# Score products of a recurrent mixer as tiles of 32 weight columns

## The chip, the cores and the metric

One NeuronCore of a Trainium2 chip runs the whole program. The metric is the device time of one execution in microseconds (us); the median of the runs counts. TensorE is called PE here, VectorE DVE, ScalarE ACT, GpSimd POOL, and SyncE SP.

## The reference, cut to what matters

Two transformer-like blocks run one after the other on 1024 tokens of 1024 features, all in fp32. The change touches one part of the first block, the HGRN2 mixer. It has 6 heads of 128 channels:

```python
# per chunk: b = cumsum(log_f); diff[t, s] = b[t] - b[s] for s <= t, else -inf
scores = jnp.einsum('bhtk,bhsk,bhtsk->bhts', qb, kb, jnp.exp(diff))
o = (jnp.einsum('bhts,bhsv->bhtv', scores, vb)
     + jnp.einsum('bhtk,bhkv->bhtv', qb * jnp.exp(b), state))
new_state = (jnp.exp(b_last[:, :, 0, :])[..., None] * state
             + jnp.einsum('bhsk,bhsv->bhkv', kb * jnp.exp(b_last - b), vb))
```

The score of a query token t and a key token s is a product over channels with the decay between s and t in it. Around the mixer stand the projection into it (w_in), a pooling mixer, the projection out (w_out) and an MLP; the second block has neighbourhood attention, a convolution and a gated MLP.

## The kernel before, in words

Activations are kept with features on the partitions and the 1024 tokens along the free axis. A projection is a `product` (L681): 8 feature tiles, each with three products of split fp32 numbers (hi x hi, lo x hi, hi x lo) for two halves of 512 tokens, so 48 matmuls for one weight tile. POOL splits each weight tile into hi and lo (L620, L622), SP loads it, two slots take turns.

The mixer computes its scores in chunks of 128 tokens, 8 chunks (`NC`), and within a chunk by levels. At level l the tokens fall into blocks of 2 << l; keys of the left half of a block meet queries of its right half, and no others. ACT copies the decayed keys and queries side by side into `e_t` (L1298, L1299, two slots, by l % 2); PE multiplies (L804); DVE copies the pairs that belong to the level into `s_t` under a mask, `pair_mask` (L1830), and meanwhile carries the decays on for the next level (`move`, L1805 to L1807). The diagonal (a token with itself) comes from k_t and q_t (L818) and is merged by L1815.

For L804, the weights of one chunk are all 128 columns of its `e_t`, keys and queries together (64 columns at level 6, whose left half holds all keys), and the streamed operand is the 64 query columns, picked by `level_parts(e, l)[:, :, 1, :]`. The result lies in 128 x 64 of a PSUM bank for each chunk, and only blocks near the diagonal are used: what the mask leaves out is never read into `s_t`. For L818 the weights are 128 columns of k_t and the stream 128 columns of q_t, though one value in each column is used.

Each of the 6 heads is one pass of `head` on PE, ACT and DVE; the first five are a loop, the last is written apart. Between its steps PE does pieces of other products (`meanwhile`, `between_steps`): project_g of this head and project_f, project_q and project_i of the next, 192 matmuls a head. The order on PE is written out by hand: project_g; L818, level 0, level 1; project_f; transposes of zv (L720), level 2, level 3; half of project_q; level 4, level 5; the other half; level 6, transposes of kd_t (L720); three parts of project_i with the state updates (L852) between; the outputs (L861, L863); the sums of squares (L869). In the last head pieces of the output projection stand in place of the next head's products; they need `h_lo`, which DVE writes at L1788 among its merge steps.

The waits around the change: PE waits for `level_ready` (ACT) before a level and for `level_merged` (DVE) where a bank is used again: levels 0, 2 and 5 use bank 4, levels 1, 3 and 6 bank 5, level 4 bank 6, L818 banks 6 and 7. After a stage its last matmul raises `level_done`.

Of the kernel before, what the change touches and what calls it, by code (L numbers as in the profile page):

```python
# [28 lines left out]
P = 128  # L29
# [13 lines left out]
CHUNK = 128  # L43
NC = SEQ // CHUNK
LEVELS = 7
MASK_W = LEVELS * CHUNK // 2 + CHUNK
D_FF = 4096
GRID_W = 64
# [97 lines left out]
def two_blocks(nc, dram, out):  # L146
    ctx = ExitStack()
    with ctx:
# [32 lines left out]
        def arena(*shapes):  # L181
# [29 lines left out]
            ("kd_tok", [P, NC, P], F32), ("states", [P, NC, P], F32), ("pool_w", [P, 2, P], F32),  # L211
            ("pair_mask", [P, MASK_W], F32))

# [55 lines left out]
        psum = ctx.enter_context(nc.psum_tensor("psum", [P, BANKS, HALF], F32))  # L269
# [391 lines left out]
        def level_parts(tile, level):  # L661

            return tile.rearrange("p (n two s) -> p n two s", two=2, s=1 << level)
# [3 lines left out]
        def _(pe):  # L667
# [49 lines left out]
            def turn(src, dst_bank, tiles, done):  # L717

                for c, block_in in enumerate(tiles):
                    last = pe.transpose(psum[:, dst_bank + c // 4, (c % 4) * P:(c % 4 + 1) * P],  # L720
                                        block_in, ident[:, :])
                last.then_inc(done, 1)
# [71 lines left out]
            def head(h, meanwhile):  # L794

                def level(l, bank):


                    pe.wait_ge(level_ready, h * LEVELS + (l + 1))

                    keys = CHUNK if l < LEVELS - 1 else CHUNK // 2
                    for c in range(NC):
                        e = e_t[:, l % 2, c * CHUNK:(c + 1) * CHUNK]
                        last = pe.matmul(psum[0:keys, bank, c * (CHUNK // 2):(c + 1) * (CHUNK // 2)], e[:, 0:keys],  # L804
                                         level_parts(e, l)[:, :, 1, :], start=True, stop=True)
                    last.then_inc(level_done, 1)

                def merged_up_to(l):

                    pe.wait_ge(level_merged, h * (LEVELS + 1) + (l + 2))  # L810

                meanwhile[0]()

                pe.wait_ge(o_scaled, h + 1)
                pe.wait_ge(k_ready, h + 1)
                pe.wait_ge(q_ready, h + 1)
                for c in range(NC):
                    last = pe.matmul(psum[:, 6 + c // 4, (c % 4) * P:(c % 4 + 1) * P],  # L818
                                     k_t[:, c * CHUNK:(c + 1) * CHUNK], q_t[:, c * CHUNK:(c + 1) * CHUNK],
                                     start=True, stop=True)  # L820
                last.then_inc(level_done, 1)

                pe.wait_ge(o_log, h + 1)
                level(0, 4)
                level(1, 5)
                meanwhile[1]()

                pe.wait_ge(zv_ready, h + 1)
                merged_up_to(-1)
                turn(zv, 6, [zv[:, c * P:(c + 1) * P] for c in range(NC)], v_turned)  # L830
                merged_up_to(0)
                level(2, 4)
                merged_up_to(1)
                level(3, 5)
                meanwhile[2]()
                pe.wait_ge(v_ready, h + 1)
                level(4, 6)
                merged_up_to(2)
                level(5, 4)
                meanwhile[3]()  # L840
                merged_up_to(3)
                level(6, 5)

                pe.wait_ge(level_moved, h * LEVELS + LEVELS)
                merged_up_to(4)
                turn(kd_t, 6, [kd_t[:, c * P:(c + 1) * P] for c in range(NC)], kd_turned)
                meanwhile[4]()

                pe.wait_ge(kd_tok_ready, h + 1)
                merged_up_to(6)  # L850
                for c in range(NC - 1):
                    last = pe.matmul(psum[:, 4 + c // 4, (c % 4) * P:(c % 4 + 1) * P], kd_tok[:, c, :],  # L852
                                     v_tok[:, c, :], start=True, stop=True)
                last.then_inc(update_done, 1)
                meanwhile[5]()

                pe.wait_ge(state_ready, h * (NC - 1) + (NC - 1))
                for c in range(NC):
                    o = psum[:, 6 + c // 4, (c % 4) * P:(c % 4 + 1) * P]
                    tokens = slice(c * CHUNK, (c + 1) * CHUNK)  # L860
                    last = pe.matmul(o, v_tok[:, c, :], s_t[:, tokens], start=True, stop=(c == 0))  # L861
                    if c >= 1:
                        last = pe.matmul(o, states[:, c, :], qd_t[:, tokens], start=False, stop=True)  # L863
                last.then_inc(o_done, 1)
                meanwhile[6]()

                pe.wait_ge(o_sq, h + 1)
                for t in range(2):
                    last = pe.matmul(psum[:, 4 + t, :], ones[:, :], e_t[:, 1, t * HALF:(t + 1) * HALF],  # L869
                                     start=True, stop=True)  # L870
                last.then_inc(o_mean, 1)
                meanwhile[7]()
# [28 lines left out]
            for j in range(2):  # L901
                pe.wait_ge(pool_p_ready, j + 1)
                for t in range(2):
                    last = pe.matmul(psum[:, 4 + 2 * j + t, :], pool_w[:, j, :],
                                     pool_p[:, j, t * HALF:(t + 1) * HALF], start=True, stop=True)
                last.then_inc(pool_mixed, 1)
            pe.wait_ge(pool_ready, 2)
            with pe.Fori(0, HEADS - 1) as i:
                head(i, between_steps(i))
# [11 lines left out]
            def begin_rest():  # L921
                begin_out(1, range(5, 7))
                begin_out(2, range(7))

            head(HEADS - 1, [lambda: project_g(HEADS - 1), lambda: begin_out(0, range(0, 4)),
                             lambda: begin_out(0, range(4, 7)), lambda: begin_out(1, [0]), lambda: begin_out(1, [1]),
                             lambda: begin_out(1, [2, 3]), lambda: begin_out(1, [4]), begin_rest])
# [247 lines left out]
            for i in range(2 * KT):  # L1175
# [5 lines left out]
                for k in range(2):  # L1181
                    at_d = slice(k * HALF + d % 4 * P, k * HALF + (d % 4 + 1) * P)
                    wh, wl = (w_hi[:, 0, at_d], w_lo[:, 0, at_d]) if d < 4 else (w_hi_last[:, at_d], w_lo_last[:, at_d])
                    for j, (w, a) in enumerate(((wh, ffn_hi_last), (wh, ffn_lo_last), (wl, ffn_hi_last))):
                        last = pe.matmul(psum[:, 4 + i % 4, :], w, a[:, k, t * HALF:(t + 1) * HALF],  # L1185
                                         start=(k == 0 and j == 0), stop=(k == 1 and j == 2))
# [11 lines left out]
        def _(act):  # L1198
# [87 lines left out]
            def head(h, last):  # L1286
                def level(l):
# [4 lines left out]
                    else:  # L1292
                        act.wait_ge(level_moved, h * LEVELS + l)
                    if l >= 2:
# [1035 lines left out]
```

## Time and profile before

| | us |
|---|---|
| median of 3 runs | 2748.89 (2746.91 to 2749.15) |
| the profiled execution | 2747.53 |
| its span | 2745.6 |
| PE busy in the span | 2660.2 (97%) |
| DVE, ACT, POOL busy | 1458.2, 643.2, 913.8 |

The span runs from the first to the last instruction of the profiled execution. Busy shares are means over the span; a stage is read from the timeline and from busy times in a stretch of it. A group of the timeline has its start, its length from the first start to the last end, and the number of records. One fp32 matmul of the code leaves two matmul records and two weight loads; a product of split numbers (L681) and a transpose leave one. The end of a matmul record lies beyond the start of the next, since matmuls are pipelined: the distance from start to start is what a record costs.

### The profile page before, as it was taken

How to read it: one execution, taken by the hardware profiler on the slowest of the kernel's cores; microseconds unless marked ns; L12 is line 12 of the kernel's file. 1: busy time of each engine (PE TensorE's matmuls, PEld its weight loads, DVE VectorE, ACT ScalarE, POOL GpSimd, SP SyncE). 2: the span in 40 equal slices, each digit the busy share in tenths (PEclk: the TensorE clock that was granted, in tenths of full speed). 3: DMA queues.
4: the chain of work that ended last, by engine and by line, in shares of the span. 5: the costliest groups of instructions: out<-in, count | busy, mean ns of one | idle time of the engine just before them, and what ended most of it. 6: DMA issues, size and time to landing. Idle time of an engine off the chain costs nothing.

```text
span 2745.6 us, 33855 instructions
## 1 busy us (share of the span) xinstructions
PE 2660.2 (97%) x12569; PEld 2195.7 (80%) x12569; DVE 1458.2 (53%) x1657; ACT 643.2 (23%) x844; POOL 913.8 (33%) x481
## 2 busy tenths in 40 slices
PE   8999999999999999999889889999999999999997
PEld 7888887888888888887667767888878888888886
DVE  7545446343433434357888886224255555555556
ACT  4233334220001010023434444001131111111113
POOL 2222222333333333333434333333333333333333
PEclk9999999999999999999999999999999999999999
DMA  5111112112112111113110001113111111111111
GB/s 201 33 37 31 31 31 85 46 50 57 53 49 60 49 46 53 46 46 116 31 37 29 21 23 46 47 46 115 46 46 47 46 53 46 46 49 51 46 46 77
DMA packets 201585, 144.96 MB, mean 53 GB/s; under 512 B 14095, under 2 KB 183738, under 8 KB 200506
## 3 DMA queue, kind: packets, MB, share of 16 engines
q1 hardware_dynamic: 189604, 122.92, 14.5%
q10 hardware_dynamic: 11926, 21.28, 2.2%
q8 instruction: 37, 0.61, 0.1%
q14 instruction: 18, 0.15, 0.0%
HBM read 131.59 MB, written 14.36 MB: 53 GB/s over the span
## 4 chain that ended last, share of the span: by engine, by line
PE 80%; DVE 14%; issue 4%; ACT 1%; DVEq 1%; DMA 0%; SPq 0%; ACTq 0%
PE psum L681 52%; PE psum L700 16%; DVE conv_t L2042 4%; PE psum L1085 3%; PE psum L804 2%; PE psum L720 2%; DVE h_lo L1685 1%; PE psum L1002 1%; DVE ffn_gate L2218 1%; DVE x_t L1939 1%; PE psum L1185 1%; PE psum L1019 1%; DVE prob L2108 1%; DVE sq_sum L1680 1%; DVE u_t L2051 0%
## 5 line engine op out<-in xcount | busy, mean ns | idle before, releaser
L620 POOL CAST w_hi<-w_raw 128x1024 fp32r<-128x1024 f32 x212 | 239.6, 1130 | 1615.7 <-issue 785.9
L681 PE MATMUL psum<-h_hi,w_hi 128*128 128x512 f32 x2384 | 754.4, 395 | 9.7 <-DVE h_lo L1788 5.4
L681 PE MATMUL psum<-h_lo,w_hi 128*128 128x512 f32 x2384 | 742.7, 391 | 0.0
L681 PE MATMUL psum<-h_hi,w_lo 128*128 128x512 f32 x2384 | 741.4, 390 | 0.0
L622 POOL TENSOR_TENSOR w_lo<-w_raw,w_hi 128x1024 fp32r<-128x1024 f32 x212 | 569.4, 2686 | 17.0
L681 PEld LDWEIGHTS psum<-h_hi,w_hi 128*128 128x128 f32 x2384 | 444.3, 189 | 107.4 <-issue 15.3
L681 PEld LDWEIGHTS psum<-h_lo,w_hi 128*128 128x128 f32 x2384 | 449.4, 188 | 94.5
L681 PEld LDWEIGHTS psum<-h_hi,w_lo 128*128 128x128 f32 x2384 | 449.2, 188 | 94.6
L1939 DVE TENSOR_TENSOR x_t<-x_t,psum 128x512 f32<-128x512 f32 x416 | 281.8, 685 | 193.2 <-PE psum L700 191.0
L2210 DVE TENSOR_TENSOR ffn_z<-psum,rinv 128x1024 f32<-128x1024 f32 x44 | 53.9, 1224 | 272.8 <-PE psum L681 267.2
L700 PE MATMUL psum<-mlp_hi,w_hi 128*128 128x512 f32 x480 | 186.7, 389 | 0.0
L700 PE MATMUL psum<-mlp_lo,w_hi 128*128 128x512 f32 x480 | 186.7, 389 | 0.0
L700 PE MATMUL psum<-mlp_hi,w_lo 128*128 128x512 f32 x480 | 186.7, 389 | 0.0
L1954 DVE SCALAR_TENSOR_TENSOR mlp_a<-psum,rinv 128x1024 f32<-128x1024 f32 x32 | 39.2, 1225 | 235.5 <-PE psum L681 229.9
L2042 DVE SCALAR_TENSOR_TENSOR conv_t<-u_t,cols,conv_t 128x1024 f32 x88 | 147.8, 1680 | 10.0 <-DVE conv_t L2037 0.6
L700 PE MATMUL psum<-ffn_hi,w_hi 128*128 128x512 f32 x320 | 126.8, 396 | 4.1 <-DVE x_t L1939 3.4
L700 PE MATMUL psum<-ffn_lo,w_hi 128*128 128x512 f32 x320 | 124.7, 390 | 0.0
L700 PE MATMUL psum<-ffn_hi,w_lo 128*128 128x512 f32 x320 | 124.7, 390 | 0.0
L633 POOL TENSOR_TENSOR conv_pool<-conv_pool,sig_cb 128x1024 f32<-128x1024 f32 x28 | 68.0, 2430 | 138.1 <-ACT sig_cb L1489 138.1
L1370 ACT ACTIVATE mlp_a<-mlp_a 128x1024 f32<-128x1024 f32 x32 | 34.0, 1062 | 305.4 <-DVE mlp_a L1954 305.4
L700 PEld LDWEIGHTS psum<-mlp_lo,w_hi 128*128 128x128 f32 x480 | 90.1, 188 | 18.7
L700 PEld LDWEIGHTS psum<-mlp_hi,w_lo 128*128 128x128 f32 x480 | 90.1, 188 | 18.7
(284 smaller groups left out, 3008.2 us busy)
## 6 DMA issues: line engine op xcount, KB each, us to landing
w_raw<-in_w_up SPq DMA_DIRECT2D x152, 256.0 KB, 3.1
w_raw<-in_w_in SPq DMA_DIRECT2D x124, 256.0 KB, 3.2
w_raw<-in_w_down SPq DMA_DIRECT2D x108, 256.0 KB, 2.8
w_raw<-in_w_out SPq DMA_DIRECT2D x32, 256.0 KB, 3.1
x_in<-in_x SPq DMA_DIRECT2D x8, 512.0 KB, 8.6
x_spill<-x_t ACTq DMA_DIRECT2D x1, 4096.0 KB, 12.3
x_spill<-x_t ACTq DMA_DIRECT2D x4, 1024.0 KB, 5.1
x_t<-x_spill ACTq DMA_DIRECT2D x1, 4096.0 KB, 12.3
```

The source lines that it names most:

```text
L620: pool.tensor_copy(hi, w_raw[:, slot, :]).then_inc(weight_hi, 1)
L622: pool.tensor_tensor(lo, w_raw[:, slot, :], hi.bitcast(F32), ALU.subtract).then_inc(weight_split, 1)
L633: pool.tensor_tensor(conv_pool[:, :], conv_pool[:, :], tap_product, ALU.add).then_inc(tap_added, 1)
L681: last = pe.matmul(psum[:, first_bank + t, :], w, a[:, k, t * HALF:(t + 1) * HALF], start=(k == 0 and j == 0), stop=(k == KT - 1 and j == 2))
L700: last = pe.matmul(psum[:, 4 + g % 4, :], w, a[:, k, t * HALF:(t + 1) * HALF], start=(k == 0 and j == 0), stop=(k == 1 and j == 2))
L720: last = pe.transpose(psum[:, dst_bank + c // 4, (c % 4) * P:(c % 4 + 1) * P], block_in, ident[:, :])
L804: last = pe.matmul(psum[0:keys, bank, c * (CHUNK // 2):(c + 1) * (CHUNK // 2)], e[:, 0:keys], level_parts(e, l)[:, :, 1, :], start=True, s ...
L1085: last = pe.matmul(psum[:, bank + t, :], w, a[:, k, t * HALF:(t + 1) * HALF], start=(k == 0 and j == 0), stop=(k == 3 and j == 2))
L1939: dve.tensor_tensor(x_d, x_d, psum[:, 4 + g % 4, :], ALU.add).then_inc(down_added, 1)
L1954: dve.scalar_tensor_tensor(mlp_a[:, j, :], banks(2 * j), 0.0, rinv[:, :], ALU.max, ALU.mult)\
L2042: dve.scalar_tensor_tensor(acc, u_t[:, tap:tap + SEQ], w, acc, ALU.mult, ALU.add)\
L2210: dve.tensor_tensor(ffn_z[:, part, :], banks(2 * part), rinv[:, :], ALU.mult).then_inc(ffn_read, 1)
```

## The change

A constant `COLS = 32` is new, and the score products are cut along the keys into groups of `width` weight columns, each written to its own partitions of the same PSUM bank. `width` is 32 for levels 0 to 4, 64 for level 5 and 32 for level 6. At levels 0 to 5 a group streams only the queries of its own tokens (`width` / 2 columns), at level 6 both groups stream all 64 queries of the chunk. The diagonal is cut into four 32 x 32 products a chunk. The number of matmuls in the code per chunk goes from 1 to 4 (diagonal, levels 0 to 4) and from 1 to 2 (levels 5 and 6). What was written outside these blocks is no longer written; the masks, the merges and all waits are as before.

```diff
+COLS = 32
...
-                    keys = CHUNK if l < LEVELS - 1 else CHUNK // 2
+                    width = min(COLS, CHUNK // 2) if l == LEVELS - 1 else max(COLS, 2 << l)
                     for c in range(NC):
-                        e = e_t[:, l % 2, c * CHUNK:(c + 1) * CHUNK]
-                        last = pe.matmul(psum[0:keys, bank, c * (CHUNK // 2):(c + 1) * (CHUNK // 2)], e[:, 0:keys],
-                                         level_parts(e, l)[:, :, 1, :], start=True, stop=True)
+                        for first in range(0, CHUNK // 2 if l == LEVELS - 1 else CHUNK, width):
+                            begin, tokens = (0, CHUNK) if l == LEVELS - 1 else (first, width)
+                            at_k = c * CHUNK + first
+                            e = e_t[:, l % 2, c * CHUNK + begin:c * CHUNK + begin + tokens]
+                            dst = psum[first:first + width, bank, (c * CHUNK + begin) // 2:(c * CHUNK + begin + tokens) // 2]
+                            last = pe.matmul(dst, e_t[:, l % 2, at_k:at_k + width], level_parts(e, l)[:, :, 1, :],
+                                             start=True, stop=True)
                     last.then_inc(level_done, 1)
...
                 for c in range(NC):
-                    last = pe.matmul(psum[:, 6 + c // 4, (c % 4) * P:(c % 4 + 1) * P],
-                                     k_t[:, c * CHUNK:(c + 1) * CHUNK], q_t[:, c * CHUNK:(c + 1) * CHUNK],
-                                     start=True, stop=True)
+                    for first in range(0, CHUNK, COLS):
+                        keys = slice(c * CHUNK + first, c * CHUNK + first + COLS)
+                        at_c = (c % 4) * P + first
+                        last = pe.matmul(psum[first:first + COLS, 6 + c // 4, at_c:at_c + COLS], k_t[:, keys], q_t[:, keys],
+                                         start=True, stop=True)
                 last.then_inc(level_done, 1)
```

## Rows read from the trace of the kernel before

**Rows 1.** The page, part 1: busy us of each engine.
```profile
PE 2660.2 (97%) x12569; PEld 2195.7 (80%) x12569; DVE 1458.2 (53%) x1657; ACT 643.2 (23%) x844; POOL 913.8 (33%) x481
```
**Rows 2.** Waits of PE: what waited, for whom, us in total, times, longest.
```profile
PE psum L1002 <- DVE k_lo L2082: 28.9, 4, 7.3
...
PE psum L681 <- DVE h_lo L1788: 5.4, 1, 5.4
```
**Rows 3.** A steady head: length, busy PE, PEld, DVE, ACT, POOL, clock, DMA share, GB/s.
```profile
161.88:227.77 65.89, 65.89 (x386) 56.75 (x385) 33.02 (x45) 22.18 (x27) 13.99 (x8) 1.00 0.11 32
```
**Rows 4.** Groups of PE by line in that head: busy us, mean ns of one.
```profile
L804 PE MATMUL psum<-e_t 128*128 128x64 f32 (+1 forms) x112 | 12.2, 266 | 0.0
```
**Rows 5.** Timeline of PE in that head: start, length, what.
```profile
162.08 1.95 PE L818 MATMUL psum<-q_t,k_t 128*128 128x128 f32 x16
...
167.36 0.71 PE L681 MATMUL psum<-h_hi,w_hi 128*128 128x512 f32 x2
167.90 0.63 PE L681 MATMUL psum<-h_lo,w_hi 128*128 128x512 f32 x2
...
179.25 3.68 PE L804 MATMUL psum<-e_t 128*128 128x64 f32 x32
...
188.28 3.68 PE L804 MATMUL psum<-e_t 128*128 128x64 f32 x32
...
196.43 0.61 PE L681 MATMUL psum<-h_lo,w_hi 128*128 128x512 f32 x2
196.88 0.61 PE L681 MATMUL psum<-h_hi,w_lo 128*128 128x512 f32 x2
197.43 1.15 PE L804 MATMUL psum<-e_t 128*64 128x64 f32 x16
198.50 1.09 PE L720 MATMUL psum<-ident,kd_t 128*128 128x128 f32 x8
```
**Rows 6.** Timeline of PE near the end: matmuls that stream one column.
```profile
2718.65 0.36 PE L1169 MATMUL psum<-ones,sq 128*128 128x1 f32 x2
2718.87 0.36 PE L1168 MATMUL psum<-ones,sq_sum 128*128 128x1 f32 x2
```
**Rows 7.** Weight loads of level 6: timeline, then durations ns min/median/max.
```profile
197.42 1.01 PEld L804 LDWEIGHTS psum<-e_t 128*64 128x64 f32 x16 [0.35 <-issue]
...
L804 PEld LDWEIGHTS psum<-e_t x14: 138/138/138, 197.5 to 198.3; 128*64 128x64 f32 x14
```
**Rows 8.** Timeline of PE, attention: two scores on two row halves, then products.
```profile
1341.94 0.53 PE L1002 MATMUL psum<-k_lo,q_hi 64*128 64x256 f32 x2
1342.15 0.53 PE L1002 MATMUL psum<-k_hi,q_lo 64*128 64x256 f32 x2
...
1343.63 1.05 PE L681 MATMUL psum<-h_lo,w_hi 128*128 128x512 f32 x2
1344.48 1.05 PE L681 MATMUL psum<-h_hi,w_lo 128*128 128x512 f32 x2
```
**Rows 9.** Timeline of PE in the last head, after level 1.
```profile
436.54 1.19 PE L681 MATMUL psum<-h_hi,w_hi 128*128 128x512 f32 x2 [5.45 <-DVE h_lo L1788]
```
**Rows 10.** The stretch behind that wait, columns as in rows 3.
```profile
436.50:441.40 4.90, 4.86 (x11) 3.45 (x12) 4.68 (x6) 4.90 (x7) 0.00 (x0) 0.50 0.11 32
```
**Rows 11.** Timeline of ACT in the steady head: k_t, and e_t of levels 1 to 3.
```profile
157.68 1.04 ACT L1313 ACTIVATE k_t<-zf 128x1024 f32<-128x1024 f32 x1
...
162.47 0.68 ACT L1299 ACTIVATE e_t<-qd_t 128x512 f32<-128x512 f32 x1
...
169.80 0.63 ACT L1299 ACTIVATE e_t<-qd_t 128x512 f32<-128x512 f32 x1
...
173.03 0.62 ACT L1299 ACTIVATE e_t<-qd_t 128x512 f32<-128x512 f32 x1
```
**Rows 12.** Timeline of POOL in that head: the start of one weight split.
```profile
197.66 1.04 POOL L620 CAST w_hi<-w_raw 128x1024 fp32r<-128x1024 f32 x1 [15.48 <-issue]
```
**Rows 13.** The page, part 3: the queue that loads instructions: packets, MB, share.
```profile
q8 instruction: 37, 0.61, 0.1%
```

## The prediction, made before the result was known

> **What bounds the kernel now.** I read the busy shares first: TensorE (PE) is busy 97% of the span, VectorE 53%, ScalarE 23%, GpSimd 33% [rows 1]. Then the waits of PE: over the whole span the longest is 28.9 us in the attention pairs, and inside the recurrent mixer there is one only, 5.4 us for h_lo [rows 2]. The change touches the mixer alone, so the stretch view matters: a steady head lasts 65.89 us with PE busy for 65.89 of them, VectorE 33.02, ScalarE 22.18, GpSimd 13.99 [rows 3]. What PE saves or loses in a head is therefore the head's gain or loss, as long as nothing else becomes late. In a head the score products (L818 and L804) hold 16 and 112, so 128 of the 386 matmul records [rows 3 to 5]. The timeline says when: L818 with levels 0 and 1 at 162.08, levels 2 and 3 at 179.25, 4 and 5 at 188.28, level 6 at 197.43 [rows 5].
>
> **What sets the pace of these records.** Each fp32 matmul of the code leaves two records, each with a weight load. From L818 at 162.08 to L681 at 167.36 are 5.28 us, and the first L681 pair is 0.09 us longer than the usual 0.45, so 48 records take 5.37 us: 0.112 us each, whether 128 (L818) or 64 columns (L804) stream [rows 5]. L1168 and L1169 stream one column each against 128 weight columns and still come every 0.112 us [rows 6]. So the weight load sets the pace. Level 6 has 64 weight columns: 16 loads in 1.01 us of which one lasts 0.138, so (1.01 - 0.138)/15 = 0.058 us each [rows 7]. 64 columns less save 0.054 us; by the same line 32 columns would take 0.031 us.
>
> **The change, part by part.**
> (a) L818 and levels 0 to 4 (six stages a head). Each had 16 records of 0.112 us = 1.79 us. Now each has 8 chunks x 4 groups x 2 = 64 records. Call p the mean distance of two records. If one column group's loads and matmuls run beside another's, each group has 16 records of 0.031 and the stage takes 0.50 us (p = 0.008). If loads go one behind the other, 64 x 0.031 = 1.98 us (p = 0.031). The row nearest to the question is the pair of scores of two heads that use different row halves of the array: their 256-column matmuls start in twos, the next two 0.21 us after them (1341.94, 1342.15), and at the same halved clock two 512-column matmuls take 0.85 us one behind the other, so 0.43 each and 0.21 for 256 columns [rows 8]. Two tiles thus did in 0.21 us what one does. Those are row tiles and not column tiles, which is what I cannot see. I take overlap, but p = 0.012 instead of 0.008, half as much again, because nothing here shows records that follow each other so closely: 64 x 0.012 = 0.77 us, a saving of 1.02 a stage, 6.13 a head. Bounds: 0.008 saves 7.7 a head, 0.016 saves 4.6, 0.031 costs 1.2, and at level 6's 0.058 it costs 11.5.
> (b) Level 5: 32 records with 64 weight columns in two groups. Overlapped 16 x 0.058 = 0.93, a saving of 0.86; one behind the other 1.86, a loss of 0.07.
> (c) Level 6: 16 records become 32 with 32 weight columns and still 64 streamed. A fp32 stream of 64 cannot be read from a row of its own, but level 6's 0.058 covers it. Overlapped 0.93 again: nothing; in line 1.86, a loss of 0.93.
> (d) Going to another tile width. Level 6 shows its price already: the L681 pair ahead takes 0.55 us to the next start where 0.45 is usual (+0.10), and the 16 records take 1.07 us to L720 where 0.93 would do (+0.14), so 0.24 a visit [rows 5]. The change adds three visits (the group of L818, level 2 with 3, level 4 with 5) and a step from 32 to 64 columns between 4 and 5, half a visit: 3 x 0.24 + 0.13 = 0.85 us a head. Bounds: 0 if the engine needn't empty, 1.7 at twice the price.
> A steady head: 6.13 + 0.86 + 0 - 0.85 = 6.1 us less, five times 30.7.
> (e) The last head. After level 1 PE waits 5.45 us for h_lo (L1788), which VectorE writes after the zg and merge steps of its own queue [rows 9]. The first group ends earlier and the wait grows: 3 x 1.02 - 0.24 = 2.8 us are lost there. It gives 6.1 - 2.8 = 3.3 us. The clock is granted at 0.50, its lower level of 1.2 GHz, in the 4.9 us after that wait [rows 10]; a longer wait may shift that stretch, for which I take nothing and keep 2 us to either side.
>
> **Cover.** L818 waits for k_t, which ends at 158.72, against a start at 162.08; level 1 for e_t ready at 163.15, 1.07 us after L818's start. With p = 0.012 level 1 would begin 0.24 + 1.54 us after it: covered; at 0.008, 1.24: just covered. Level 2 waits for its e_t (170.43), level 3 for its own (173.65), with VectorE's merges of levels 0 and 1 between; they would begin about 3 us earlier than 179.25 and 181.0: covered. These four are ScalarE's ends in [rows 11]. e_t of levels 4 and 5 follows steps of PE that come earlier by as much, and each has a product of 24 records, 5.4 us, in front of it. GpSimd idles 15.5 us before it splits a weight tile [rows 12]; heads 6 us shorter leave that. VectorE's 33 us fit a head of 60. So no other wait takes the place of PE's work, unless the saving passes 10 us.
>
> **Sum.** 5 x 6.1 + 3.3 = 34 us. The profiled execution took 2747.5 us (span 2745.6), and the median of the runs is 1.4 above it. 2747.5 - 34 = 2713.5 in its terms, 2715 against the median. At p = 0.008 it is 42 us (2707), at 0.016 26 us (2723).
>
> **What the skill adds.** Rows 8 show two tiles at work at once, and no row shows column tiles. The Trainium skill, "TensorEngine Tiling (Array Packing)", Key Properties, says that different tiles load weights and multiply in parallel; "TensorE: Matmul & The Clock Gate", Part 3, puts about 4 ns between the starts of tiles, by which p would be the 0.008 that the groups' own loads give, and the time 2707. The same page, Part 2 (back-to-back issue gap), gives about 25 ns as the least distance of two matmuls and speaks against the change: by it a stage would take 1.6 us and the time would be 2743; that is rival B. Its 62 ns per matmul with hardware decode off doesn't fit level 6's 58 [rows 7].
>
> **The rivals.**
> A. The loads stay in one line (slower). All column groups are fed by one load path and each record costs 0.031 us: a head has (a) -1.2, (b) -0.07, (c) -0.93, (d) -0.85 = 3.0 us more; in the last head 0.8 us of it vanish in the wait. 5 x 3.0 + 2.2 = 17 us: 2766. It decides from p = 0.028 on, where six stages no longer save anything. For it: in all rows of the mixer a load starts only behind the matmul before it, and 128 and 64 columns cost in proportion, as if one path were the limit. Against it: the pair in [rows 8].
> B. Records have a price of their own between 0.02 and 0.028 us, whatever their width. With (b) to (d) near zero together, the gain is 5 x 6 x (1.79 - 64 p), with half of it for the last head: at p = 0.025, 6 us (2743). For it: nothing in the trace comes closer than that. Against it: nothing either, but L1168 shows that a matmul of one column adds nothing to the load's pace.
> C. The pair of load and matmul costs level 6's 0.058 us however narrow. A stage is 3.7 us, a head (a) -11.5, (b), (c), (d) as in A: 13.4 us more; the last about 8: 75 us, 2824. Against it: 64 columns take half of 128's time, so at 64 the width still rules.
> D. The loop body grows from 386 to 386 - 128 + 448 = 706 record pairs. The queue of instructions moves only 37 packets, 0.61 MB, in the whole span [rows 13], so loops are not fetched anew on each round; if the longer body were, or if thin tiles let the clock fall to 0.50 around them, some 5 us a head: about 2745 with the gain of (a). Nothing in the profile speaks for it; the clock stays at 1.00 in steady heads [rows 3].
>
> **Chances.** Forecast (p up to 0.018) 0.54; between it and B, still faster, 0.08; B 0.08; A 0.20; C 0.07; D 0.03. The likeliest case's own range is 2705 to 2727. To leave out no more than 2 in 10 the range must reach A: 2704 to 2770, leaving out C and the tails. About 0.2% (5.5 us) is what a measurement can tell from no change. Faster by more than that: forecast, the part behind it and a little of B, 0.63; within 0.2%: 0.07; slower: A, C and some of D, 0.30.
>
> **What would show it.** Right: between L818's first start and the next L681 some 2.6 us instead of 5.3, level 6 near 1.1 us, heads of 60 us with PE still busy throughout, and a wait for h_lo near 8 us. Wrong: the group takes 6 us or more (A, C), or PE waits appear in front of L804 (the cover failed), or L681 groups spread beyond 0.45 us a pair (clock). If starts of tiles of different groups never lie closer than 0.03 us, step (a) is wrong.

## The result, and the profile after

The changed kernel takes 2715.91 us (median of 4 runs, 2713.68 to 2716.54) against 2749.02 us before (4 runs, 2746.91 to 2750.23): ratio 0.9879, 95% interval 0.9862 to 0.9896. The forecast was 2715. The profiled execution has a span of 2713.7 us, 31.9 less than before. PE is as busy as it was, part 1 of the page after (busy us, share, records):

```profile
PE 2624.4 (97%) x14489; PEld 2152.1 (79%) x14489; DVE 1464.4 (54%) x1657; ACT 643.0 (24%) x844; POOL 915.2 (34%) x481
```

So 1920 more records (6 heads x 320), and less time. The busy times of a steady head after (length, busy PE, PEld, DVE, ACT, POOL, granted clock, DMA share, GB/s) stand against [rows 3]:

```profile
157.04:215.96 58.92, 58.92 (x705) 48.77 (x704) 34.10 (x45) 22.12 (x28) 14.44 (x8) 1.00 0.12 36
```

The head fell from 65.89 to 58.92 us, PE has no gap in it, the clock is 1.00. Its score stages in the timeline of PE (start, length, what) answer to [rows 5]:

```profile
156.49 0.61 PE L682 MATMUL psum<-h_hi,w_lo 128*128 128x512 f32 x2
157.04 0.76 PE L826 MATMUL psum<-q_t,k_t 128*32 128x32 f32 x64
157.64 1.31 PE L809 MATMUL psum<-e_t 128*32 128x16 f32 x128
158.88 0.74 PE L682 MATMUL psum<-h_hi,w_hi 128*128 128x512 f32 x2
159.46 0.63 PE L682 MATMUL psum<-h_lo,w_hi 128*128 128x512 f32 x2
...
170.91 1.41 PE L809 MATMUL psum<-e_t 128*32 128x16 f32 x128
172.25 0.74 PE L682 MATMUL psum<-h_hi,w_hi 128*128 128x512 f32 x2
...
177.93 1.80 PE L809 MATMUL psum<-e_t 128*32 128x16 f32 x96
179.67 0.74 PE L682 MATMUL psum<-h_hi,w_hi 128*128 128x512 f32 x2
...
185.37 1.09 PE L809 MATMUL psum<-e_t 128*32 128x64 f32 x32
186.39 1.09 PE L721 MATMUL psum<-ident,kd_t 128*128 128x128 f32 x8
```

From start to start: diagonal with levels 0 and 1 took 5.28 us and takes 1.84, levels 2 and 3 3.49 and now 1.34, levels 4 and 5 3.49 and now 1.74 (the x96 are both levels: the group keeps the name of its first form), level 6 1.07 and now 1.02. Together 13.33 and 5.94, so 7.39 less, of which 0.42 go to the edges: the L682 pair ahead of a stage takes 0.54 or 0.55 to the next start and the first one behind it 0.58, where 0.45 is usual. That is the head's 6.97.

Where the 31.9 us of the two profiled executions come from, by the start of L869 (now L876) in each head: the first head reaches it 5.14 us earlier, the next four gain 6.97 each (27.9), the last head loses 0.5 (59.28 us from the fifth head's L869 to its own before, 59.80 after), and the rest, from there to the end of the span, loses 0.6 (2274.7 and 2275.2). The waits of PE in the mixer after (us in total, times, longest) show that the last head is not what it was in [rows 2]:

```profile
PE psum L682 <- DVE h_lo L1795: 6.6, 1, 6.6
PE psum L809 <- ACT e_t L1306: 2.2, 1, 2.2
PE psum L809 <- issue: 2.1, 1, 2.1
```

Its timeline on PE, from level 1 on:

```profile
396.63 0.30 PE L809 MATMUL psum<-e_t 128*32 128x16 f32 x12 [2.11 <-issue]
403.53 1.19 PE L682 MATMUL psum<-h_hi,w_hi 128*128 128x512 f32 x2 [6.59 <-DVE h_lo L1795]
...
418.62 0.73 PE L809 MATMUL psum<-e_t 128*32 128x16 f32 x64
421.57 1.12 PE L809 MATMUL psum<-e_t 128*64 128x32 f32 x32 [2.22 <-ACT e_t L1306]
...
423.20 0.99 PE L682 MATMUL psum<-h_lo,w_hi 128*128 128x512 f32 x2
...
424.97 1.88 PE L809 MATMUL psum<-e_t 128*32 128x64 f32 x32
```

Level 5 waits 2.2 us for its operand, and level 6 takes 1.8 us where a steady head takes 1.02. The granted clock says why level 6 is slow. Two stretches of the last head, then one of start-up after and the same one before, columns as in [rows 3]:

```profile
399.40:409.60 10.20, 6.07 (x14) 4.35 (x15) 9.70 (x11) 9.76 (x12) 1.27 (x1) 0.50 0.23 67
...
423.30:426.60 3.30, 3.30 (x37) 2.45 (x35) 2.20 (x5) 0.73 (x2) 0.00 (x0) 0.50 0.84 333
```
```profile
48.00:58.00 10.00, 8.08 (x25) 5.40 (x25) 3.43 (x6) 3.46 (x3) 0.00 (x0) 0.83 0.92 345
...
48.00:58.00 10.00, 8.08 (x33) 6.06 (x33) 4.17 (x7) 3.46 (x3) 0.48 (x1) 1.00 0.94 353
```

A second stretch at half clock follows the new wait. In start-up, ahead of anything that the change touches, this execution had the clock at 0.83 in the ten microseconds from 48, the one before at 1.00, and its first head began at 98.07 instead of 96.17: that accounts for the 1.8 us by which the first head's L876 gained less than the others. It is not the change: of the other profiled executions the three with half clock near 50 us (by_group, wide_stream, cols64) begin their first head at 97.55 to 98.00, all the rest at 95.74 to 96.55.

### The profile page after: what moved, and what is told of

Read it like the earlier page. It is cut to its first block, busy times and chain, and to the rows that moved or that the text cites. A ratio compares the mean times of both kernels' runs of the same rounds, so it can differ in the third digit from the quotient of the medians.

```text
span 2713.7 us, 37695 instructions
## 1 busy us (share of the span) xinstructions
PE 2624.4 (97%) x14489; PEld 2152.1 (79%) x14489; DVE 1464.4 (54%) x1657; ACT 643.0 (24%) x844; POOL 915.2 (34%) x481
## 4 chain that ended last, share of the span: by engine, by line
PE 80%; DVE 14%; issue 4%; ACT 1%; DVEq 1%; DMA 0%; SPq 0%; ACTq 0%
PE psum L682 53%; PE psum L701 16%; DVE conv_t L2049 4%; PE psum L1092 3%; DVE h_lo L1692 2%; PE psum L721 1%; PE psum L1009 1%; PE psum L809 1%; DVE ffn_gate L2225 1%; DVE x_t L1946 1%; PE psum L1192 1%; DVE prob L2115 1%; PE psum L1026 1%; DVE sq_sum L1687 1%; DVE u_t L2058 0%
## 5 line engine op out<-in xcount | busy, mean ns | idle before, releaser
L682 PE MATMUL psum<-h_hi,w_hi 128*128 128x512 f32 x2384 | 755.5, 396 | 10.9 <-DVE h_lo L1795 6.6
L682 PE MATMUL psum<-h_lo,w_hi 128*128 128x512 f32 x2384 | 743.5, 391 | 0.0
L682 PE MATMUL psum<-h_hi,w_lo 128*128 128x512 f32 x2384 | 742.4, 391 | 0.0
L682 PEld LDWEIGHTS psum<-h_hi,w_hi 128*128 128x128 f32 x2384 | 444.8, 189 | 109.3 <-issue 16.4
L682 PEld LDWEIGHTS psum<-h_lo,w_hi 128*128 128x128 f32 x2384 | 449.8, 189 | 94.9
L682 PEld LDWEIGHTS psum<-h_hi,w_lo 128*128 128x128 f32 x2384 | 449.5, 189 | 94.9
L701 PEld LDWEIGHTS psum<-mlp_hi,w_hi 128*128 128x128 f32 x480 | 90.1, 188 | 18.7
```

What stands on the lines that cost most here:

```text
L682: last = pe.matmul(psum[:, first_bank + t, :], w, a[:, k, t * HALF:(t + 1) * HALF], start=(k == 0 and j == 0), stop=(k == KT - 1 and j == 2))
L701: last = pe.matmul(psum[:, 4 + g % 4, :], w, a[:, k, t * HALF:(t + 1) * HALF], start=(k == 0 and j == 0), stop=(k == 1 and j == 2))
```

## Experiments

**1. Is it the column groups, or are narrow records just cheap?** (extra_one_group)

```diff
                 for c in range(NC):
                     for first in range(0, CHUNK, COLS):
...
+                        pe.matmul(psum[0:COLS, 6 + c // 4, at_c:at_c + COLS], k_t[:, keys], q_t[:, keys],
+                                  start=True, stop=True)
+                for c in range(NC):
+                    for first in range(0, CHUNK, COLS):
...
```


> Edit on the changed kernel: ahead of the diagonal's 64 records the same 64 are issued once more, all with output partitions 0 to 31, so in one column group; the real ones overwrite them. Nothing else changes. Theory 1, each column group is a line of its own and lines run side by side: in one line a record costs the narrow weight load, 0.031 us, so the extra stage takes 64 x 0.031 = 2.0 us and a steady head goes from 58.9 to 60.9 us. Theory 2, narrow records are simply cheap and the groups don't matter: the extra stage takes as long as the real one, 0.5 to 0.6 us, and the head 59.5 us.

Measured (2730.1 us, one run; steady heads 60.86 to 60.97). Timeline of PE, L826 the extra stage, L832 the real one:

```profile
160.66 2.18 PE L826 MATMUL psum<-q_t,k_t 128*32 128x32 f32 x63
...
162.71 0.75 PE L832 MATMUL psum<-q_t,k_t 128*32 128x32 f32 x61
163.29 0.29 PE L809 MATMUL psum<-e_t 128*32 128x16 f32 x13
```

In one group 64 records take 2.05 us, 0.032 each; the same records over four groups take 0.58 behind them. Theory 1 holds and theory 2 falls. The 0.031 that was drawn as a line through 128 and 64 columns is right too. This kernel showed one thing more. In the last head it has the 2.1 us of "issue" of the changed kernel too (2.17), and a new one of the kind in the first head, with none in the heads between:

```profile
98.55 1.32 PE L809 MATMUL psum<-e_t 128*32 128x16 f32 x128
102.15 0.64 PE L682 MATMUL psum<-h_hi,w_hi 128*128 128x512 f32 x2 [2.28 <-issue]
```

PE stands still for 2.28 us with nothing to wait for that the profile knows.

**2. Does the order of issue matter?** (by_group, then two_in_a_row)

```diff
-                    for c in range(NC):
-                        for first in range(0, CHUNK // 2 if l == LEVELS - 1 else CHUNK, width):
+                    for first in range(0, CHUNK // 2 if l == LEVELS - 1 else CHUNK, width):
+                        for c in range(NC):
...
```

The two loops of the diagonal are swapped likewise.

> Edit on the changed kernel: the two loops are swapped, so that all 8 chunks of one column group are issued before the next group (16 record pairs of one group in a row). Same matmuls, same results. Theory 1a, lines side by side and TensorE looks further ahead than 16 pairs: stages stay at 0.6 us, head 58.9. Theory 1b, lines side by side but it looks ahead over a few records only: consecutive records are of one group and queue at 0.031 us, a 32-column stage takes about 2.0 us, level 5 1.9, level 6 1.8, and the head grows by 6 x 1.4 + 0.9 + 0.8 = 10 us to 69 us. Theory 2 (groups don't matter): 58.9.

Measured: 2758.6 us (one run), slower than the 2749.1 of before beside it; heads of 66.76 us. Timeline of PE, two stages (levels 2 and 3):

```profile
181.81 3.52 PE L809 MATMUL psum<-e_t 128*32 128x16 f32 x128
185.26 0.72 PE L682 MATMUL psum<-h_hi,w_hi 128*128 128x512 f32 x2
```

3.45 us for two stages, 1.7 each against 1.79 before the change: the gain is gone with the same matmuls. Theory 1b was right; its 2.0 us a stage and 69 us a head were too much, as the groups overlap a little where they meet. The starts of single records show the rest: within a group they follow at 31 to 32 ns, and only around the change of group do about four loads of either group alternate. I read that as a look-ahead over three or four waiting pairs, and tested it:

```diff
-                    for c in range(NC):
-                        for first in range(0, CHUNK // 2 if l == LEVELS - 1 else CHUNK, width):
+                    for pair in range(0, NC, 2):
+                        for c, first in [(c, first) for first in range(0, CHUNK // 2 if l == LEVELS - 1 else CHUNK, width)
+                                         for c in (pair, pair + 1)]:
...
```

The diagonal has the same order here.

> Edit on the changed kernel: two chunks of the same column group are issued in a row before the next group (4 record pairs of one group instead of 2). Same matmuls, same results. by_group showed that the next group's records start only while the last three or four of the former are open. If TensorE looks past about four waiting pairs, two lines are busy at a time instead of four: a 32-column stage takes about 1.0 us instead of 0.6, and a head 58.9 + 6 x 0.4 + a little for levels 5 and 6 = 61.5 us. If the look-ahead is longer than 12 pairs, nothing changes; if groups of 4 serialize as in by_group, stages take 1.65 and the head 66.8.

Measured: 2723.6 us (one run), heads of 59.30 to 59.35 us, 0.4 more than the changed kernel, not 2.6 more. The same two stages:

```profile
228.98 1.58 PE L810 MATMUL psum<-e_t 128*32 128x16 f32 x128
230.49 0.73 PE L682 MATMUL psum<-h_hi,w_hi 128*128 128x512 f32 x2
```

1.51 against 1.34. A common look-ahead of four pairs would have kept two groups busy, and this falls. What fits all three orders is that each column group takes in some four pairs of its own, and the issue stops at the first pair whose group is full: runs of 2 and 4 pairs pass, a run of 16 holds up the others. That is an inference; no run counts the depth by itself.

**3. Load or stream as the pace of a group?** (wide_stream)

```diff
-                            begin, tokens = (0, CHUNK) if l == LEVELS - 1 else (first, width)
+                            begin, tokens = (0, CHUNK) if l != LEVELS - 2 else (first, width)
```


> Edit on the changed kernel: at levels 0 to 4 each group of 32 weight columns streams all 64 queries of its chunk instead of its own 16; the added results are masked out. Theory 1 with the load as the pace of a line: the fp32 stream of 64 (level 6 shows 0.058 with its load) now sets it, 16 x 0.055 = 0.88 us a stage instead of 0.5 to 0.6, five stages: a head of about 60.7 us. Theory 2 or a pace set by the issue of records: no change, 58.9. If the lines shared one stream path, 64 x 0.053 = 3.4 us a stage: 73 us.

Measured: 2725.0 us (one run), heads of 60.6 us, as theory 1 had it. Levels 0 and 1:

```profile
159.03 2.12 PE L809 MATMUL psum<-e_t 128*32 128x64 f32 x128
161.09 0.73 PE L682 MATMUL psum<-h_hi,w_hi 128*128 128x512 f32 x2
```

1.03 us a stage, 0.064 for each of a group's 16 records, with 64 columns streamed, against 0.62 with 16. Four groups stream 64 columns each in a third of the 3.4 us that one path would take. The stream is the limit there, the load in the change.

**4. The price of a visit to another tile width.** (level6_wide on the kernel before, diag_only on the changed one)

```diff
-                    keys = CHUNK if l < LEVELS - 1 else CHUNK // 2
+                    keys = CHUNK
```


> Edit on the kernel before: level 6 takes 128 weight columns like the other levels, so the one visit to a narrower tile disappears from the head of 65.89 us. Its 16 records go from 0.058 to 0.112 us each, +0.86 us. If a visit costs 0.24 us as I read it, the head grows by 0.62 to 66.5; if a visit is free, by 0.86 to 66.75.

Measured: 2754.1 us (one run), heads of 66.40 us, +0.51. PE around level 6:

```profile
197.43 1.89 PE L804 MATMUL psum<-e_t 128*128 128x64 f32 x16
199.15 1.04 PE L720 MATMUL psum<-ident,kd_t 128*128 128x128 f32 x8
```

The wider loads cost 0.86, so the visit that went was worth 0.35, not 0.24. diag_only puts the old code of all levels back and keeps the tiles of L826:

> Edit on the changed kernel: only the diagonal (k_t, q_t) is cut into 32-column tiles; all levels are as before the change. Its 64 records take 64 x 0.0079 = 0.50 us instead of 1.79, -1.29 us, and there is one visit more. With the visit at 0.35 us, as level6_wide gives it, a head takes 65.89 - 0.94 = 64.95 us; with my 0.24 it takes 64.84; with a free visit 64.6.

Measured: heads of 64.99 us:

```profile
226.51 0.76 PE L822 MATMUL psum<-q_t,k_t 128*32 128x32 f32 x64
227.20 3.79 PE L805 MATMUL psum<-e_t 128*128 128x64 f32 x32
230.80 0.71 PE L682 MATMUL psum<-h_hi,w_hi 128*128 128x512 f32 x2
```

-0.90 where the loads alone give -1.29: 0.39 for the visit, if the stage itself takes 0.50. So 0.35 to 0.39 from two sides. Its whole time was 2747.8 us, one run: what follows the last head (from its sums of squares to the end) took 2279.4 us in this execution and 2274.7 in the profiled one of before, and hid the five heads' 4.5 us. A single total can't tell this; the heads can.

**5. Width against number.** (cols64)

```diff
-COLS = 32
+COLS = 64
```


> Edit on the changed kernel: COLS = 64, so every stage has two groups of 64 weight columns with 32 records, and level 6 one group as before the change. By lines side by side with the load as pace: 16 x 0.058 = 0.93 us a stage instead of the 0.50 of 32 columns, six stages, less 0.15 for the step between levels 4 and 5: a head of 58.92 + 2.6 - 0.15 = 61.3 us. If the number of records set the pace (0.009 each), 32 records take 0.3 us and the head gets shorter, 57 us.

Measured: 2725.4 us (one run), heads of 60.87 us.

```profile
158.42 1.15 PE L826 MATMUL psum<-q_t,k_t 128*64 128x64 f32 x32
159.40 2.01 PE L809 MATMUL psum<-e_t 128*64 128x32 f32 x64
161.34 0.73 PE L682 MATMUL psum<-h_hi,w_hi 128*128 128x512 f32 x2
```

0.97 to 0.98 a stage: half the records, two thirds more time. The weight columns that one group must load set the pace, not the records. The forecast was 0.4 us too high, as the 32-column stages take 0.60 and not 0.50.

**6. What the profile after points to.** (narrow5, last_order, both)

```diff
-                            dst = psum[first:first + width, bank, (c * CHUNK + begin) // 2:(c * CHUNK + begin + tokens) // 2]
-                            last = pe.matmul(dst, e_t[:, l % 2, at_k:at_k + width], level_parts(e, l)[:, :, 1, :],
+                            cols = min(width, COLS)
+                            dst = psum[first:first + cols, bank, (c * CHUNK + begin) // 2:(c * CHUNK + begin + tokens) // 2]
+                            last = pe.matmul(dst, e_t[:, l % 2, at_k:at_k + cols], level_parts(e, l)[:, :, 1, :],
```


> Edit on the changed kernel: level 5 takes only the 32 keys of each block's left half as weights (2 groups of 32 columns instead of 2 of 64); what it no longer computes is masked out anyway. By lines side by side: 16 x 0.031 = 0.50 us instead of 16 x 0.058 = 0.93, and no step from 32 to 64 columns any more (0.13 to 0.18): a steady head goes from 58.92 to about 58.35, five heads 2.9 us, the last head nothing, since there level 5 waits for its e_t: about 2713 us, ratio to before 0.987. If the pace of level 5 were set by the number of records (32 either way), nothing changes: 2716.

Measured: 2714.05 us (2710.04 to 2714.40), ratio to before 0.9862 (0.9845 to 0.9878). Heads of 58.4 to 58.5 us; levels 4 and 5 take 1.31 us instead of 1.74:

```profile
175.75 1.38 PE L810 MATMUL psum<-e_t 128*32 128x16 f32 x96
177.06 0.74 PE L682 MATMUL psum<-h_hi,w_hi 128*128 128x512 f32 x2
```

The number of records is the same and their time is not, so the weight columns set the pace here as well. The head lost 0.1 us less than forecast, as a 32-column stage takes 0.6 us and not 0.50.

last_order touches the last head alone:

```diff
...
                 level(4, 6)
+                if ahead_of_5 is not None:
+                    ahead_of_5()
                 merged_up_to(2)
                 level(5, 4)
...
-            def begin_rest():
-                begin_out(1, range(5, 7))
...
-                             lambda: begin_out(0, range(4, 7)), lambda: begin_out(1, [0]), lambda: begin_out(1, [1]),
-                             lambda: begin_out(1, [2, 3]), lambda: begin_out(1, [4]), begin_rest])
+                             lambda: begin_out(0, range(4, 7)), lambda: begin_out(1, [2]), lambda: begin_out(1, [3]),
+                             lambda: begin_out(1, [4, 5]), lambda: begin_out(1, [6]), begin_rest],
+                 ahead_of_5=lambda: begin_out(1, [0, 1]))
```


> Edit on the changed kernel: in the last head alone two parts of the second output tile (12 matmuls, 2.7 us) are done between levels 4 and 5, and the later parts move up by as much. Theory a, the last head gave less than forecast because PE waited 2.2 us for level 5's e_t and the clock fell after it: level 5 starts when its operand is ready, 1.5 to 2 us are gained, up to 3.5 with the clock: 2712 to 2714.5 us. Theory b, the end of the last head is set by VectorE's queue anyway: the wait comes back in front of level 6 or the transposes, 2716.

Measured: 2714.31 us (2711.86 to 2714.52), ratio 0.9865 (0.9848 to 0.9881). The last head takes 58.90 us to its sums of squares (L876 in the changed kernel, L878 here) instead of 59.80:

```profile
416.88 0.74 PE L809 MATMUL psum<-e_t 128*32 128x16 f32 x64
420.51 1.12 PE L809 MATMUL psum<-e_t 128*64 128x32 f32 x32
423.15 1.09 PE L809 MATMUL psum<-e_t 128*32 128x64 f32 x32
```

No wait in front of level 5, and level 6 at full clock. The list of waits has a new one, 1.2 us of L682 for e_t (L1356) behind the head: the work moved forward is missing there. The 0.9 us understate the gain, because 2.7 us of work more lie ahead of the sums of squares. Up to one and the same matmul of the output projection behind both, the last head takes 57.33 us from its first stage instead of 59.47: 2.1 us less, the new wait included, as theory a had it. Theory b holds only for that wait. The median moved 1.6 us, within the spread of the runs.

> The edits of narrow5 and last_order together. If they are independent, the gains add: 2.9 + 1.5 to 3.5 us, 2709.5 to 2711.5 us.

Measured: 2712.93 us (2712.45 to 2716.33), ratio 0.9862 (0.9845 to 0.9878): above the range expected. So the changed kernel and this one ran once more side by side.

> The changed kernel itself, unedited, in one call with both_again, so that the two share a chip and the runs of before. About 2715.5 us; heads of 58.92 us again. What varies is the share of low clock in start-up and in the attention stage, some us.

> The kernel of both (level 5 with 32 weight columns, two output parts between levels 4 and 5 of the last head) once more, beside the changed kernel. By its steady heads (58.47 against 58.92) and its last head (58.50 against 59.80) it should be 5 x 0.45 + 1.3 = 3.5 us faster than after_again, if what follows the mixer is alike.

Measured: 2716.03 us (2712.94 to 2718.02) for the changed kernel, 2711.78 (2710.72 to 2716.21) for the other; against the same runs of before 0.9870 (0.9854 to 0.9887) and 0.9862 (0.9844 to 0.9879). The medians are 4.3 us apart, with 3.5 expected. The two profiled executions are 5.2 us apart: steady heads of 58.37 to 58.42 against 58.79 to 58.85 give 2.1 of it, and the last head 3.6 up to the same matmul (to the sums of squares 58.49 against 60.84). The last head of the changed kernel was slower in this execution than in the first (60.84 against 59.80), so part of the 3.6 is chance. The ranges of the runs overlap. The kernel has the lowest median of the study, but the ratios of narrow5, last_order and this one (0.9862, 0.9865, 0.9862) can't be told apart, and their intervals overlap with that of the change.

## Why the prediction was right, point by point

**PE bounds the heads.** Right: the heads shortened by what the stages lost, and PE has no gap in them.

**(a) Column groups run side by side.** Right in kind (experiments 1 and 3). I took 0.012 us a record; the single starts of a stage give 0.0085 on the mean of its first half and 0.0094 of its second. 64 x 0.009 = 0.58 us instead of 0.77: 7.3 us a head, not 6.1, and the first group takes 1.84 us, not 2.6. The lower bound that the rows gave was nearly reached; the half that I added for an unseen issue limit wasn't there. On the starts: the 25 ns between matmuls that the Trainium skill gives ("TensorE: Matmul & The Clock Gate", Part 2) don't hold between column groups: starts lie 6 to 12 ns apart at the beginning of a stage and later by turns 1 to 2 and 14 to 17, 9 on the mean. That is nearer to the 4 ns of its Part 3.

**(b), (c).** Right: level 5 takes 1.06 with the step before it, forecast 0.93 + 0.13; level 6 1.02.

**(d) The price of a visit.** Mis-sized: 0.35 to 0.39 instead of 0.24 (experiment 4), so 3.5 visits are 1.2 to 1.4 us a head and not 0.85. I counted what the narrow stage and the pair ahead of it lost, and not that the first wide load behind it is delayed as well (the 0.58 of the L682 pair). The Trainium skill, "TensorEngine Tiling (Array Packing)", Key Properties, says that a change of mode drains TensorE; the delay on both edges agrees with it. (a) and (d) together: forecast 6.1 with (b), measured 6.97 a head.

**(e) The last head.** This step failed: forecast a gain of 3.3 us, measured a loss of 0.5, and of 1.6 in the second profiled execution of the same kernel (after_again, 60.84 us). The 5.45 us wait grew as said, to 6.6 and 2.1 more ahead of it (8.7, forecast 8.3). But the Cover part looked at a steady head only. In the last head VectorE also writes h_lo, and level 5's e_t hangs on its queue. Level 5's e_t on ACT and levels 4 and 5 on PE before, then that e_t after:

```profile
453.84 0.61 ACT L1299 ACTIVATE e_t<-qd_t 128x512 f32<-128x512 f32 x1
...
453.15 3.68 PE L804 MATMUL psum<-e_t 128*128 128x64 f32 x32
```
```profile
420.82 0.61 ACT L1306 ACTIVATE e_t<-qd_t 128x512 f32<-128x512 f32 x1
```

The head's first stage began at 425.63 before and at 392.72 after, so this e_t was ready 28.8 and 28.7 us behind it: the change did not move it. Before, PE came to level 5 at 29.2; now it came at 26.6 and waited 2.2 us. The end of the first wait, counted the same way, didn't move either (10.9 and 10.8 us). So VectorE's queue and not PE's work sets the pace of this head up to level 5, and what PE saves there is lost. And the clock, which I let stand for 2 us either way, cost more: half clock over 10.2 us instead of 6.8 around the first wait, and over 3.4 us more after the second, 6.8 in after_again. The clock's share shows in wide_stream and cols64: their steady heads are slower, but in the last one they waited only 1.7 us in front of level 5, had half clock over 6.8 us around the first wait and none behind the second, and took 58.51 us, less than the change. last_order removes the second wait and the low clock behind it and gives back 2.1 us (experiment 6).

**Rival A** (one load path) and **B, C** fell with experiment 1. But A is what happens inside one group, and by_group shows that a poor order of issue brings nearly all of it back. **Rival D** was right about the code: the instruction queue moved 42 packets instead of 37, and the 2.1 us of "issue" in the last head and 2.28 in the first head of extra_one_group fall where code is passed for the first time; the other heads of the loop have no such gap. A block of 16 KB was on its way when the gap of the last head began (from 394.18 for 0.97 us), which fits. The other runs say more: in all eight executions whose last head issues 64 diagonal and 128 level records in turns, PE stops ahead of the same record, the 181st of the head, and goes on 3.9 to 4.3 us after the head's start. by_group has the same records there, but passes them so slowly that it comes to this one after 4.6 us, and it has no gap. So the supply of instructions is the likely cause; no run takes code alone away. In the change the gap hid under the wait for h_lo.

**The sum.** 34 us forecast, 33.1 between the medians, 31.9 between the profiled executions. That it came out so close was in part luck. The steady heads gave 6.97 us each instead of 6.1, 4.3 us more in five; the last head gave 3.8 us less than forecast, the low clock in start-up took 1.8, and what follows the mixer 0.6. The point value is better than its terms.

## What to carry to other kernels

Small fp32 products whose pace is the weight load gain from column tiles where the result is block-diagonal: the price is (weight columns of one group) x (records of one group), so cut until groups are narrow, and drop columns that the mask discards. This holds while few columns are streamed: with 64 a record of a group takes 0.064 us and not 0.032. Issue the groups in turn, never one group's work in a row. Count every change of tile width at 0.35 us here, and check the odd pass of a loop, above all the last, on its own: its waits are others than those of a steady pass.

## What the runs showed that I had not expected

The order of issue alone moved the same matmuls from 58.9 to 66.8 us a head, while four in a row cost only 0.4. The first pass through thin records stalled for 2.1 to 2.5 us, most likely on code, as they use up instructions far faster than wide ones. And the half-clock stretches behind waits differ from execution to execution, in start-up and in the attention stage too: what follows the sums of squares of the last head, the same work in all kernels without the edit of last_order, took from 2274.7 to 2281.9 us in the profiled executions, more than some effects looked for.
